# Forty up-projection pairs by Strassen's scheme on one core: seven half-size products, weight sums by adding transfers, g through DRAM, one separate down-projection

## The chip, the core and the metric

The kernel runs on one core of one Trainium2 chip. The metric is device time in microseconds (us) of the whole program, one launch. TensorE (PE in the profile) multiplies, VectorE (DVE), ScalarE (ACT) and GpSimd (POOL) work element by element, SyncE (SP) and GpSimd's queue (POOLq) issue transfers, which run on 16 DMA engines.

## The reference

One layer of a residual block, 512 tokens, width 2048, all in float32. The change touches its second sub-layer, the gated MLP:

```python
h2 = rmsnorm(x, ffn_pre_g)
up = causal_depthwise_conv(h2 @ w_up, conv_f_w, conv_f_b)      # w_up (2048, 11264), conv over 3 tokens
u_gate, u_val = jnp.split(up, 2, axis=-1)                      # 5632 columns each
f = (jax.nn.gelu(u_gate, approximate=True) * u_val) @ w_down   # w_down (5632, 2048)
x = x + rmsnorm(f, ffn_post_g)
```

Ahead of it stands a token-mixing sub-layer (w_in, w_a_out, w_b_out, w_o), behind it a per-layer embedding (w_ple, w_ple_gate). They are the same in both kernels.

## The kernel before

**Three products for one.** Every float32 matmul is made of three passes in the reduced type fp32r: an operand is split into a rounded high part and the rest, and high times high, high times low and low times high are summed in PSUM. Weights come in units of 128 partitions x 1024 float32 (512 KB; eight chunks of 128x128, or two of 128x512). For every unit ScalarE writes `w_hi` (`split`, L639), VectorE writes `w_lo = w_raw - w_hi` (`split`, L944), and TensorE makes 24 matmuls of it, 8 chunks x 3 (`products`, L400 to L402; `rows`, L466 to L468 for the down-projection). SyncE loads unit u when VectorE has split unit u-1 (two raw buffers); ScalarE splits unit u+4 when TensorE has finished unit u (four `w_hi` slots). So a split has about three units' time before TensorE wants it.

**The order of the work** is written out by hand, one program for each engine, with semaphores between them. The MLP goes over 44 column pairs, each a 128-wide column of the gate half and one of the value half, in 11 groups of four (`up`, then `down` for the group before). One column of 2048 rows is two units, 48 matmuls of 512 tokens; a pair is 96. Per column VectorE scales the PSUM tile by the token factors (`scale_tile`, L948), ScalarE makes the first tap of the convolution (L838), VectorE the other two (`last_taps`, L1275 and L1278). ScalarE makes the gelu (L843), VectorE the product (L1285); ScalarE (L834) and VectorE (L969) split the product g into high and low. Per group `down` multiplies four chunks of g by 8 units of w_down and VectorE adds the 16 PSUM tiles to `f_acc` (L1316), which GpSimd has set to zero (`memset`, L377).

**Ahead of the first pair** (`first_pair`) the second residual `x2` is turned by TensorE, squared row by row (L654), and its token factors go through four `diag` tiles (L959) and a matmul with ones (`spread`, L478). GpSimd stores `x2` in DRAM (L373), waits for it, and then sets `f_acc` to zero.

Of the kernel before, what the change touches and what calls it, by code (L numbers as in the profile page):

```python
# [34 lines left out]
P = 128  # L35
# [33 lines left out]
U_L = U_F + 4 * FC + 8 * NGRP  # L69
# [9 lines left out]
T_G = T_F + 2 * FC + DC * NGRP  # L79
F_UP = lambda j: U_F if j == 0 else U_F + 4 * GRP + 24 * (j - 1)  # L80
F_DOWN = lambda j: U_F + 4 * GRP + 24 * j + (4 * GRP if j < NGRP - 1 else 0)
FT_UP = lambda j: T_F if j == 0 else T_F + 2 * GRP + 24 * (j - 1)
FT_DOWN = lambda j: T_F + 2 * GRP + 24 * j + (2 * GRP if j < NGRP - 1 else 0)
# [15 lines left out]
C_ALL = C_CFW + FTAPS * 2 * FC  # L99

# [48 lines left out]
def build(nc, x, p, mix_pre_g, w_in, conv_a_w, conv_a_b, ln_a_g, ln_a_b, w_a_out, pool_w, pool_scale, w_b_out,  # L149
          w_o, mix_post_g, ffn_pre_g, w_up, conv_f_w, conv_f_b, w_down, ffn_post_g, w_ple, w_ple_gate,  # L150
          ple_post_g, out):
    x2_dram = nc.dram_tensor("x2_dram", (P, NG, BLK, W), F32, kind="Internal").ap()
    rows_of = lambda a: a.rearrange("a (b t) (n f) -> t n (a b) f", t=P, f=W)
    ctx = ExitStack()
    with ctx:
# [43 lines left out]
        g_hi = place("g_hi", [P, 2, GRP, TOK], F32R, r4)  # L199
        g_lo = place("g_lo", [P, 2, GRP, TOK], F32R, r4 + FULL // 2)  # L200
# [13 lines left out]
        gain_f = place("gain_f", [P, NG, W], F32, r2 + FULL - 4 * D)  # L214
# [8 lines left out]
        diag = small("diag", [P, BLK, P])  # L223
        r_bc = small("r_bc", [P, TOK])
        sq = small("sq", [P, 2, TOK])
# [4 lines left out]
        conv_acc = small("conv_acc", [P, TOK])  # L230
        sums = small("sums", [P, BLK, NG])
# [10 lines left out]
        raw_in = [sem(f"raw_in{s}") for s in range(RAW)]  # L242
        slots_freed = sem("slots_freed")
        hi_ready, lo_ready, units_done = sem("hi_ready"), sem("lo_ready"), sem("units_done")
# [19 lines left out]
        ff_ready, g_hi_ready, g_ready = sem("ff_ready"), sem("g_hi_ready"), sem("g_ready")  # L264
        ple_taken, y_ready = sem("ple_taken"), sem("y_ready")
        x_back, x2_out, f_zero = (sem(n) for n in ("x_back", "x2_out", "f_zero"))
# [9 lines left out]
        def _(sp):  # L276
            for_k = lambda w: w.rearrange("(k p) n -> p k n", p=P)
            win, wa, wb, wo = for_k(w_in), for_k(w_a_out), for_k(w_b_out), for_k(w_o)
            wup, wdn, wpg, wpl = for_k(w_up), for_k(w_down), for_k(w_ple_gate), for_k(w_ple)
# [15 lines left out]

            def pair(u, w, cols):

                for h in range(2):
                    for j in range(2):
                        half_column(u + (2 * h + j), w, cols[j], h)  # L300
# [33 lines left out]
            pair(At(F_UP(0)), wup, (0, FF))  # L334
            with sp.Fori(1, GRP) as c:
                column(At(F_UP(0), c, 4), wup, c * P)
                column(At(F_UP(0) + 2, c, 4), wup, c * P + FF)
            with sp.Fori(0, NGRP - 1) as j:
                for c in range(GRP):
                    column(At(F_UP(1) + 4 * c, j, 24), wup, j * (GRP * P) + (GRP + c) * P)  # L340
                    column(At(F_UP(1) + 4 * c + 2, j, 24), wup, j * (GRP * P) + ((GRP + c) * P + FF))
                for n in range(NG):
                    for v in range(GRP // 2):
                        rows(At(F_DOWN(0) + 2 * n + v, j, 24), wdn, j * GRP + 2 * v, n)
            with sp.Fori(0, NG) as n:
# [14 lines left out]
        def _(pool):  # L360
# [1092 lines left out]
```

## Time and profile before

| | us |
|---|---|
| median of 3 runs | 2665.03 |
| lowest, highest | 2664.44, 2666.41 |
| span of the profiled execution | 2665.0 |

| engine | busy us | share of the span | instructions |
|---|---|---|---|
| TensorE, matmul | 2637.8 | 99% | 11714 |
| TensorE, weight load | 2184.9 | 82% | 11714 |
| VectorE | 1348.2 | 51% | 1693 |
| ScalarE | 806.5 | 30% | 972 |
| GpSimd | 13.5 | 1% | 34 |

The span of the profiled execution equals the median, so a sum made against the profile needs no correction. The DMA engines move 277 MB, 104 GB/s on the mean. Weight loads have a row of their own (PEld) and overlap the matmuls. The recorded duration of a matmul (389 ns) is its latency; matmuls follow each other faster than that, and the distance of their starts is what counts.

### The profile page before, as it was taken

Reading aid. Unit: us, or ns where it says so; the run is one execution under the profiler, and the core shown is the slowest. Engines: PE = TensorE matmul, PEld = TensorE weight load, DVE = VectorE, ACT = ScalarE, POOL = GpSimd, SP = SyncE. Lnnn points to the kernel's source line nnn. Section 1 sums busy time; section 2 is a strip of 40 time slices with the busy share of each in tenths; the row PEclk is TensorE's granted clock in tenths of the full one; section 3 lists DMA queues with packets and bytes.
Section 4 is the critical chain, followed back from the end, with each engine's and each line's share of the span. In section 5 each row is a group of like instructions: output and inputs, shape, how many; then the busy total and the mean of one; then the engine's idle time right before and its main releaser. Section 6 shows DMA issues by size and latency. Waiting matters only on the chain.

```text
span 2665.0 us, 31629 instructions
## 1 busy us (share of the span) xinstructions
PE 2637.8 (99%) x11714; PEld 2184.9 (82%) x11714; DVE 1348.2 (51%) x1693; ACT 806.5 (30%) x972; POOL 13.5 (1%) x34
## 2 busy tenths in 40 slices
PE   8999999999999999999999999999999999999998
PEld 7888888888888877888888888888888888888886
DVE  6888766643334237444445444444454444446534
ACT  5222322342223234332323232222222222224423
POOL 0000000000000001000000000000000000000000
PEclk9999999999999999999999999999999999999999
DMA  5333333333334324333333333333333333343332
GB/s 163 103 95 100 98 95 99 91 115 99 95 95 161 100 79 150 95 95 98 100 95 95 97 101 96 95 96 101 96 95 96 101 97 95 96 172 103 104 103 103
DMA packets 384842, 277.26 MB, mean 104 GB/s; under 512 B 8116, under 2 KB 337500, under 8 KB 383708
## 3 DMA queue, kind: packets, MB, share of 16 engines
q1 hardware_dynamic: 380512, 259.03, 32.3%
q0 software_dynamic: 1296, 12.06, 1.2%
q10 hardware_dynamic: 2924, 4.54, 0.5%
q8 instruction: 89, 1.46, 0.2%
q14 instruction: 21, 0.17, 0.0%
HBM read 267.21 MB, written 8.39 MB: 103 GB/s over the span
## 4 chain that ended last, share of the span: by engine, by line
PE 98%; DVE 1%; ACT 1%; DMA 0%; issue 0%; DVEq 0%; ACTq 0%
PE ps L400 22%; PE ps L402 22%; PE ps L401 22%; PE ps L466 10%; PE ps L468 10%; PE ps L467 10%; PE ps L428 1%; ACT squares_out L654 0%; DVE e_buf L977 0%; DVE diag L959 0%; DMA x_nat<-in_x 0%; PE ps L478 0%; ACT xg_hi L659 0%; DVE x L977 0%; DVE w_lo L944 0%
## 5 line engine op out<-in xcount | busy, mean ns | idle before, releaser
L944 DVE TENSOR_TENSOR w_lo<-w_raw,w_hi 128x1024 fp32r<-128x1024 f32 x478 | 585.0, 1225 | 1186.1 <-ACT w_hi L639 1185.6
L400 PE MATMUL ps<-xg_hi,w_hi 128*128 128x512 f32 x2304 | 899.6, 390 | 1.6 <-DVE w_lo L944 1.6
L402 PE MATMUL ps<-xg_hi,w_lo 128*128 128x512 f32 x2304 | 898.1, 390 | 0.0
L401 PE MATMUL ps<-xg_lo,w_hi 128*128 128x512 f32 x2304 | 898.0, 390 | 0.0
L639 ACT ACTIVATE w_hi<-w_raw 128x1024 fp32r<-128x1024 f32 x478 | 506.0, 1060 | 1129.7 <-PE ps L402 599.2
L400 PEld LDWEIGHTS ps<-xg_hi,w_hi 128*128 128x128 f32 x2304 | 433.6, 188 | 92.5 <-issue 1.8
L402 PEld LDWEIGHTS ps<-xg_hi,w_lo 128*128 128x128 f32 x2304 | 433.5, 188 | 90.2
L401 PEld LDWEIGHTS ps<-xg_lo,w_hi 128*128 128x128 f32 x2304 | 433.6, 188 | 89.8
L466 PE MATMUL ps<-w_hi,g_hi 128*128 128x512 f32 x704 | 273.9, 389 | 0.0
L468 PE MATMUL ps<-w_lo,g_hi 128*128 128x512 f32 x704 | 273.9, 389 | 0.0
L467 PE MATMUL ps<-w_hi,g_lo 128*128 128x512 f32 x704 | 273.9, 389 | 0.0
L468 PEld LDWEIGHTS ps<-w_lo,g_hi 128*128 128x128 f32 x704 | 132.1, 188 | 27.5
L467 PEld LDWEIGHTS ps<-w_hi,g_lo 128*128 128x128 f32 x704 | 132.1, 188 | 27.4
L466 PEld LDWEIGHTS ps<-w_hi,g_hi 128*128 128x128 f32 x704 | 132.1, 188 | 27.3
L1316 DVE TENSOR_TENSOR f_acc<-f_acc,ps 128x512 f32<-128x512 f32 x176 | 109.0, 681 | 0.5 <-PE ps L468 0.5
L466 PE MATMUL ps<-w_hi,x_hi 128*128 128x512 f32 x256 | 99.9, 390 | 0.8 <-DVE x_lo L969 0.8
L466 PE MATMUL ps<-w_hi,xg_hi 128*128 128x512 f32 x256 | 99.7, 389 | 0.1
L468 PE MATMUL ps<-w_lo,x_hi 128*128 128x512 f32 x256 | 99.6, 389 | 0.0
L468 PE MATMUL ps<-w_lo,xg_hi 128*128 128x512 f32 x256 | 99.6, 389 | 0.0
L467 PE MATMUL ps<-w_hi,xg_lo 128*128 128x512 f32 x256 | 99.6, 389 | 0.0
L467 PE MATMUL ps<-w_hi,x_lo 128*128 128x512 f32 x256 | 99.6, 389 | 0.0
L1027 DVE SCALAR_TENSOR_TENSOR conv_acc<-a_conv,par,conv_acc 128x512 f32<-128x512 f32 x120 | 89.7, 748 | 0.0
(165 smaller groups left out, 1830.3 us busy)
## 6 DMA issues: line engine op xcount, KB each, us to landing
w_raw<-in_w_up SPq DMA_DIRECT2D x176, 512.0 KB, 3.9
w_raw<-in_w_in SPq DMA_DIRECT2D x112, 512.0 KB, 3.7
w_raw<-in_w_down SPq DMA_DIRECT2D x88, 512.0 KB, 3.7
w_raw<-in_w_o SPq DMA_DIRECT2D x32, 512.0 KB, 3.7
w_raw<-in_w_ple_gate SPq DMA_DIRECT2D x32, 512.0 KB, 3.7
w_raw<-in_w_b_out SPq DMA_DIRECT2D x16, 512.0 KB, 3.9
w_raw<-in_w_a_out SPq DMA_DIRECT2D x16, 512.0 KB, 4.0
x_nat<-in_x SPq DMA_DIRECT2D x4, 1024.0 KB, 9.6
```

Of the source, the lines that this page charges most:

```text
L400: pe.matmul(o, w_hi[:, s, cols], hi, start=start, stop=False)
L401: pe.matmul(o, w_hi[:, s, cols], lo, start=False, stop=False)
L402: return pe.matmul(o, w_lo[:, s, cols], hi, start=False, stop=stop)
L428: mm = pe.transpose(ps[:, bank0 + q, b * P:(b + 1) * P], src[:, n, b, q * P:(q + 1) * P], ident[:])
L466: pe.matmul(o, x_hi[:, k, tok], w_hi[:, s, cols], start=k == 0, stop=False)
L467: pe.matmul(o, x_lo[:, k, tok], w_hi[:, s, cols], start=False, stop=False)
L468: last = pe.matmul(o, x_hi[:, k, tok], w_lo[:, s, cols], start=False, stop=k == chunks - 1)
L639: f(w_hi[:, u.slot(SLOTS)], w_raw[:, u.slot(RAW)], ACT.Copy).then_inc(hi_ready, 1)
L944: dve.tensor_tensor(w_lo[:, s], w_raw[:, u.slot(RAW)], as_f32(w_hi[:, s]), ALU.subtract).then_inc(lo_ready, 1)
L1027: op(dve.scalar_tensor_tensor(out=both[k % 2], in0=chunk(k), scalar=weight, in1=both[k % 2], op0=ALU.mult, op1=ALU.add))
L1316: dve.tensor_tensor(f_acc[:, n, b], f_acc[:, n, b], ps[:, 4 * (n % 2) + b], ALU.add).then_inc(tiles_taken, 1)
```

## The change

**Layout.** The host hands w_up over in another order: unit by unit, so that each of the 128 rows of a transfer is 4 KB in one piece (no arithmetic).

**The first four pairs** are computed as before. Beside them VectorE makes four sums of halves of the activations (`s1`, `s2`, `s3`, `s7`, each 128 x 8 x 256) in nine instructions of 2048 columns, and splits each with ScalarE: four `low_sum` of 2048 columns on VectorE, four copies on ScalarE. TensorE waits for all four (`s_split`) before it goes on.

**The other 40 pairs** go by the Strassen-Winograd scheme. Activations are cut by halves of the 2048 rows and by halves of the 512 tokens, a pair's weights into gate and value column and halves of the rows. In place of eight products of a unit with 256 tokens (four units x 512 tokens) there are seven: W22, W11, T1, T2, T3, T4, W21. W22, W11 and W21 are units of w_up. T1 is a sum of two, T2 of three, T3 of two, T4 = T2 + W21. T1, T2 and T3 are made while they are loaded: SyncE loads one unit, GpSimd's queue issues a transfer that adds the next to it in SBUF (`add_unit`, four of them for a pair). VectorE makes T4 (`fourth_sum`). Raw units now live in a ring of ten buffers (`ring_raw`), which also hold the low parts; a buffer is loaded again when TensorE has finished the unit ten earlier. VectorE combines the seven PSUM results, with the copy `p1` that ScalarE makes, in seven instructions of 256 columns, and scales gate and value in SBUF.

**g through DRAM.** The product g is no longer split at once but stored (`g_dram`, 256 KB for a pair), read back in 11 pieces of 1 MB and split then (`quad_high`, `quad_low`). The down-projection stands behind all pairs, in four passes over 3, 3, 3 and 2 of these pieces; `f_acc` takes 64 PSUM tiles in place of 176, the first pass by copy, so the memset of `f_acc` is gone. All loops of this part are unrolled.

```diff
+W22, W11, T1, T2, T3, T4, W21 = range(PRODUCTS)
+RING = 10
+PASSES = (3, 3, 3, 2)
...
+            def ring_free(n):
+                if n < 4:
+                    sp.wait_ge(squares_ready, Q_O + DC)
...
+                else:
+                    sp.wait_ge(units_done, U_S + n - RING + 1)
...
+            for g in range(NS):
+                n, gate, val = PRODUCTS * g, GRP + g, FC + GRP + g
+                load_unit(n + W22, w_up[val, 1])
+                load_unit(n + W11, w_up[gate, 0])
+                load_unit(n + T1, w_up[val, 0])
+                load_unit(n + T2, w_up[val, 0])
+                load_unit(n + T3, w_up[val, 0])
+                load_unit(n + W21, w_up[gate, 1])
...
+            for g in range(NS):
+                n = PRODUCTS * (g + 1)
+                if g < NS - 1:
+                    add_unit(n + T1, w_up[GRP + g + 1, 0])
+                    add_unit(n + T2, w_up[GRP + g + 1, 0])
+                    add_unit(n + T3, w_up[FC + GRP + g + 1, 1])
+                    add_unit(n + T2, w_up[FC + GRP + g + 1, 1], second=True)
+                if g > 0:
+                    store_product(GRP + g - 1)
...
-            nc.gpsimd.memset(f_acc[:], 0.0).then_inc(f_zero, 1)
...
+                for k in range(HC):
+                    cols = slice(k * P, (k + 1) * P)
+                    pe.matmul(o, w_hi[:, s, cols], hi(k), start=k == 0, stop=False)
+                    pe.matmul(o, w_hi[:, s, cols], lo(k), start=False, stop=False)
+                    mm = pe.matmul(o, w_low[:, cols], hi(k), start=False, stop=k == HC - 1)
+                mm.then_inc(units_done, 1)
+
+            pe.wait_ge(s_split, 4)
+            for g in range(NS):
+                for idx in range(PRODUCTS):
+                    product(g, idx)
...
+                if c == GRP - 1:
+                    fourth_sum(0)
+                    low_sum(s2_lo, s2_raw, s2_hi, 2)
+                step(u + 3)
...
+                if c == GRP - 1:
+                    low_sum(s3_lo, s3_raw, s3_hi, 3)
```

VectorE in the third and fourth pair, before (L944 is the weight split, L1275 and L1278 the taps, L1285 the product, L969 the low part of g, L948 the scaling):

```order
L944 TENSOR_TENSOR w_lo<-w_raw,w_hi 128x1024 [waits hi_ready]
L1275 SCALAR_TENSOR_TENSOR gate_c<-up_gate,par,gate_c 128x512 [waits first_tap_ready]
L1278 SCALAR_TENSOR_TENSOR gate_c<-up_gate,par,gate_c 128x512 [waits dve_chain]
L944 TENSOR_TENSOR w_lo<-w_raw,w_hi 128x1024 [waits hi_ready]
L948 TENSOR_TENSOR up_val<-ps,r_bc 128x512
```

The same place now (L1223 and L1228 are the weight split, L1612 to L1622 the activation sums `s2` and `s3`, L1254 the low part of a sum):

```order
L1560 SCALAR_TENSOR_TENSOR gate_c<-up_gate,par,gate_c 128x512 [waits first_tap_ready,tiles_taken]
L1564 SCALAR_TENSOR_TENSOR gate_c<-up_gate,par,gate_c 128x512 [waits dve_chain]
L1612 TENSOR_TENSOR s_raw<-xg_lo,s_raw 128x2048 [waits s_ready]
L1614 TENSOR_TENSOR s_raw<-s_raw,xg_hi 128x2048 [waits dve_chain]
L1223 TENSOR_TENSOR w_lo<-w_raw,w_hi 128x1024 [waits hi_ready]
L1620 TENSOR_TENSOR s_raw<-xg_lo,s_raw 128x2048 [waits s_ready]
L1622 TENSOR_TENSOR s_raw<-s_raw,xg_hi 128x2048 [waits dve_chain]
L1233 TENSOR_TENSOR up_val<-ps,r_bc 128x512
L1228 TENSOR_TENSOR ring_lo_145<-ring_raw_135,w_hi 128x1024 [waits hi_ready]
L1560 SCALAR_TENSOR_TENSOR val_c<-up_val,par,val_c 128x512 [waits first_tap_ready,tiles_taken]
L1564 SCALAR_TENSOR_TENSOR val_c<-up_val,par,val_c 128x512 [waits dve_chain]
L1573 TENSOR_TENSOR gelu_g<-gelu_g,val_c 128x512 [waits gelu_ready,dve_chain]
```

Four instructions of 2048 columns stand between the taps of the third pair and the first weight split for the new scheme; the four low parts follow among the splits of the fourth pair.

VectorE in one of the 40 pairs now, from the results of one pair to those of the next (L1584 is `fourth_sum`, L1672 and L1722 combine the gate tile, L1714 the value tile):

```order
L1714 TENSOR_TENSOR up_val<-ps,v_115 128x256
L1716 TENSOR_TENSOR up_val<-up_val,r_bc 128x512 [waits c_taken]
L1584 TENSOR_TENSOR ring_raw_136<-ring_raw_144,ring_raw_137 128x1024 [waits units_done,ring_in2,ring_added9]
L1228 TENSOR_TENSOR ring_lo_153<-ring_raw_143,w_hi 128x1024 [waits hi_ready]
L1722 TENSOR_TENSOR up_gate<-ps,v_116 128x256 [waits c_taken,units_done]
L1672 TENSOR_TENSOR up_gate<-ps,p_113 128x256 [waits units_done]
L1228 TENSOR_TENSOR ring_lo_154<-ring_raw_144,w_hi 128x1024 [waits hi_ready]
L1677 TENSOR_TENSOR up_gate<-up_gate,r_bc 128x512 [waits c_taken]
L1560 SCALAR_TENSOR_TENSOR val_c<-up_val,par,val_c 128x512 [waits first_tap_ready,val_scaled]
```

The sum for T4 waits for adding transfers and stands ahead of a weight split in VectorE's queue.

## Rows read from the trace of the kernel before

**Rows 1.** The page: busy time and its share, by engine.
```profile
PE 2637.8 (99%) x11714; PEld 2184.9 (82%) x11714; DVE 1348.2 (51%) x1693; ACT 806.5 (30%) x972; POOL 13.5 (1%) x34
```
**Rows 2.** The page: chain that ended last.
```profile
PE 98%; DVE 1%; ACT 1%; DMA 0%; issue 0%; DVEq 0%; ACTq 0%
```
**Rows 3.** Timeline of TensorE, middle of the pairs: start, duration, engine, line.
```profile
1399.95 0.39 PE L400 MATMUL ps<-xg_hi,w_hi 128*128 128x512 f32 x1
...
1402.67 0.39 PE L400 MATMUL ps<-xg_hi,w_hi 128*128 128x512 f32 x1
```
**Rows 4.** Groups by form: line, xcount, busy us, mean ns, idle before.
```profile
L466 PE MATMUL ps<-w_hi,g_hi 128*128 128x512 f32 x704 | 273.9, 389 | 0.0
L540 PE MATMUL ps<-acc,ones 128*128 128x512 f32 x2 | 1.0, 592 | 0.0
```
**Rows 5.** Timelines of TensorE and its weight loads, at `spread` and at two float32 matmuls.
```profile
46.88 0.86 PEld L478 LDWEIGHTS ps<-diag,ones 128*128 128x128 f32 x7
...
499.32 1.02 PE L540 MATMUL ps<-acc,ones 128*128 128x512 f32 x2
...
532.86 0.86 PEld L546 LDWEIGHTS ps<-ones,acc 128*128 128x128 f32 x7
```
**Rows 6.** Timeline ahead of and at the first pairs: VectorE, TensorE, GpSimd, ScalarE.
```profile
1024.54 1.92 ACT L654 ACTIVATE squares_out<-x 128x2048 f32<-128x2048 f32 x1
...
1026.79 6.94 POOL L377 MEMSET f_acc<- 128x8192 f32 x1 [12.25 <-DMA x_dram<-x]
...
1027.12 7.13 DVE L959 TENSOR_SCALAR diag<-ident,rstd 128x128 f32<-128x128 f32 x4
...
1031.30 1.06 ACT L639 ACTIVATE w_hi<-w_raw 128x1024 fp32r<-128x1024 f32 x1 [1.76 <-DMA w_raw<-in_w_up]
...
1034.31 2.08 PE L478 MATMUL ps<-diag,ones 128*128 128x128 f32 x8 [3.30 <-DVE diag L959]
...
1036.45 0.68 DVE L965 COPY r_bc<-ps 128x512 f32<-128x512 f32 x1
...
1057.49 0.69 DVE L948 TENSOR_TENSOR up_val<-ps,r_bc 128x512 f32<-128x512 f32 x1
...
1098.13 1.06 ACT L639 ACTIVATE w_hi<-w_raw 128x1024 fp32r<-128x1024 f32 x1 [1.01 <-PE ps L402]
```
**Rows 7.** Stretches: us, busy of each engine, PEclk, DMA share, GB/s.
```profile
1016.00:1024.00 8.00, 8.00 (x43) 6.86 (x42) 3.91 (x6) 7.82 (x9) 0.00 (x0) 1.00 0.99 404
1033.40:1040.20 6.80, 5.89 (x18) 5.02 (x19) 5.83 (x12) 2.10 (x2) 0.32 (x1) 0.50 0.49 139
```
**Rows 8.** Timeline of VectorE in the pairs, middle of the kernel.
```profile
1403.96 1.23 DVE L944 TENSOR_TENSOR w_lo<-w_raw,w_hi 128x1024 fp32r<-128x1024 f32 x1 [2.58 <-ACT w_hi L639]
1405.11 0.68 DVE L948 TENSOR_TENSOR up_val<-ps,r_bc 128x512 f32<-128x512 f32 x1
...
1410.62 0.75 DVE L1275 SCALAR_TENSOR_TENSOR val_c<-up_val,par,val_c 128x512 f32<-128x512 f32 x1
...
1412.39 0.69 DVE L1285 TENSOR_TENSOR ff_prod<-gelu_g,val_c 128x512 f32<-128x512 f32 x1
...
1415.99 0.68 DVE L969 TENSOR_TENSOR g_lo<-ff_prod,g_hi 128x512 fp32r<-128x512 f32 x1
1416.59 0.69 DVE L948 TENSOR_TENSOR up_gate<-ps,r_bc 128x512 f32<-128x512 f32 x1
```
**Rows 9.** Groups of ScalarE between 1100 and 2380 us.
```profile
L639 ACT ACTIVATE w_hi<-w_raw 128x1024 fp32r<-128x1024 f32 x235 | 249.3, 1061 | 477.3 <-PE ps L468 263.9 <-PE ps L402 208.9 <-DMA w_raw<-in_w_down 4.5
L838 ACT ACTIVATE val_c<-up_val,par 128x512 f32<-128x512 f32 x41 | 33.4, 816 | 83.4 <-DVE up_val L948 83.4
L843 ACT ACTIVATE gelu_g<-gate_c 128x512 f32<-128x512 f32 x40 | 25.3, 632 | 114.1 <-DVE gate_c L1278 114.1
```
**Rows 10.** DMA issues: xcount, KB each, median us to landing.
```profile
w_raw<-in_w_up SPq DMA_DIRECT2D x176, 512.0 KB, 3.9
...
x<-x_dram POOLq DMA_DIRECT2D x4, 1024.0 KB, 5.1
```
**Rows 11.** Timeline of GpSimd: one issue of a transfer.
```profile
2369.49 0.53 POOL L384 DMA_DIRECT2D x<-x_dram  x1
```

More of the change, by code:

```diff
@@ L78 @@
 T_F = T_O + DC
[L79 to L83, printed above, removed]
+T_D = T_F + 2 * GRP
+T_G = T_D + DC * len(PASSES)
 EARLY = 7
@@ L99, with loads, adds, landed @@
 C_ALL = C_CFW + FTAPS * 2 * FC
+def loads(n):
+    return 1 if n >= N_DOWN or n % PRODUCTS != T4 else 0
+def adds(n):
+    return {T1: 1, T2: 2, T3: 1}.get(n % PRODUCTS, 0) if n < N_DOWN else 0
+def landed(n):
+    return 16 * sum(loads(m) for m in range(n % RING, n + 1, RING))
+def added(n):
+    return 16 * sum(adds(m) for m in range(n % RING, n + 1, RING))
 class At:
@@ L586, in _ @@
[L586 to L602 removed]
+            up(At(U_F), At(T_F), first=True)
@@ L604, in _ @@
+            for q in range(len(PASSES)):
+                for n in range(NG):
+                    if q == len(PASSES) - 1 and n == 1:
+                        pe.wait_ge(p_ready, PLEC)
+                    down(q, n)
             for n in range(NG):
@@ new lines, in _ @@
+            for c in range(GRP):
+                u = At(U_F + 4 * c)
+                if c == 0:
+                    step(u + 2)
+                    step(u + 3)
+                    tap_of_tile(gate_c, up_gate, c, 0)
+                    gelu(c)
+                else:
+                    step(u)
+                    step(u + 1)
+                    tap_of_tile(gate_c, up_gate, c, 0)
+                    step(u + 2)
+                    gelu(c)
+                    step(u + 3)
+                if c == 2:
+                    high_sum(s1_hi, s1_raw, 0)
+                    high_sum(s7_hi, s7_raw, 1)
+                tap_of_tile(val_c, up_val, c, 1)
+                if c == 2:
+                    high_sum(s2_hi, s2_raw, 2)
+                    high_sum(s3_hi, s3_raw, 3)
@@ new lines, in _ @@
+            for g in range(NS):
+                n, before = PRODUCTS * g, GRP + g - 1
+                if g > 0:
+                    step_ring(n - 1)
+                    val_tap(before)
+                    step_ring(n)
+                    gate_tap(before)
+                else:
+                    step_ring(n)
+                step_ring(n + 1)
+                if g > 0:
+                    act.wait_ge(c_taken, PRODUCTS * g)
+                f(p1[:], ps[:, W11, 0:TOKH], ACT.Copy).then_inc(p1_ready, 1)
+                step_ring(n + 2)
+                if g > 0:
+                    gelu(before)
+                step_ring(n + 3)
+                step_ring(n + 4)
+                if g == NS - 1:
+                    quad_high(0)
+                step_ring(n + 5)
```

620 lines of the change are left out of this document (439 added, 181 removed).

## The prediction

> **What bounds the kernel now.** I read the busy shares first [rows 1]: TensorE's matmuls fill 99% of the span, VectorE half of it, ScalarE 30%. The chain that ended last says the same: 98% of it is TensorE [rows 2]. So almost every us of matmul time taken away shows in the end, as long as nothing else becomes the limit, and almost every us in which TensorE idles is lost. How fast matmuls follow each other is read from a timeline: from 1399.95 to 1402.67 us there are 12 distances, so one matmul of 512 columns every 226.7 ns, although each is recorded with 389 [rows 3]. 512 columns at 2.4 GHz are 213.3 ns, so 13.4 ns come on top. The down-projection has the same form and the same 389 ns [rows 4]. The changed kernel keeps all of it but the 40 pairs, and alters what TensorE waits for at the two ends of them.
>
> **1. The products.** Removed are 40 pairs x 96 = 3840 matmuls of 512 columns: 3840 x 0.2267 = 870.5 us. Added are 40 x 7 x 24 = 6720 matmuls of 256 columns. The trace has no fp32r matmul of 256 columns, so their distance has to be bounded.
> - From below: each matmul brings a weight load. At L546 the matmuls have one column, so only the loads count: seven loads cover 0.86 us, and with 0.19 for the last that is 0.67/6 = 111.7 ns each [rows 5]. At `spread` (L478) seven loads take the same 0.86 us, and there the array works too: a float32 matmul of 512 columns takes 1.02 - 0.59 = 0.43 us per record [rows 4, 5], so one of 128 columns a quarter, 107 ns, just what 256 columns of fp32r take at 2.4 GHz. Load and array work of 107 ns each thus overlap at 111.7. Total 750.6 us.
> - From above: the 13.4 ns are a fixed price of a matmul: 106.7 + 13.4 = 120.1 ns, 807.1 us. If they grow with the columns instead, it is 113.4.
>
> I take 116 ns, about the middle, since no row tells fixed from growing: 779.5 us, 19.5 us for a pair where there were 21.8. The term is -91.0 us (bounds -119.9 and -63.4).
>
> The Trainium skill (TensorE: Matmul & The Clock Gate, section Back-to-back issue gap) gives columns/2.4 + 2.5 ns for a warm isolated matmul. By it 256 columns would take 109.2 ns, and the 512 of this kernel 215.8 where the row has 226.7; with 109.2 the term would be -136.7 us.
>
> **2. The start of the new scheme.** TensorE waits for the four split activation sums, and the last low part is behind the whole VectorE queue of pairs three and four. So I date that queue. A VectorE instruction of 512 columns is followed by the next after 0.60 us, one of 1024 after 1.15 [rows 8]; so 2.25 for 2048. Before, VectorE has scaled the second pair's value tile at 1057.5 + 0.6 = 1058.1 [rows 6]. That comes earlier now. The four `diag` took 7.1 us, with GpSimd's memset running all that time, and the memset is gone; but the next step still waits for a weight split that ScalarE ends at 1032.4, so `r_bc` comes at about 33.6 and not 36.45: 2.8 us. The absent splits of g (VectorE's low part, and ScalarE's copy ahead of its weight split) give about another 2.1 in this stretch, an estimate. So the queue below begins at 1053.2:
> - nine sums and four low parts, 13 x 2.25 = 29.3
> - eight weight splits, 8 x 1.15 = 9.2, and the fourth sum 1.15
> - four pairs of taps, 1410.62 to 1412.39, 4 x 1.77 = 7.1; two products 1.3; three scalings 1.8
> - waits for ScalarE: 2.0 in the third pair (tap and split), and 5.7 at the head of the fourth (tap 0.82, two copies of 2048 columns at 1.92, split 1.06) [rows 6, 9]
>
> That is 57.6 us, and TensorE starts at about 1110.8. Before, it goes on at 1098.1 [rows 6]. So +12.7 us, although the removed memset lets TensorE reach that point 6 us earlier: the 3.3 us idle at `spread` and the slow clock behind it are gained and lost again. TensorE idles some 18 us there. After the 3.3 us idle the granted clock was 0.50, the lower level, for 6.8 us [rows 7]; something like it will follow here, at half speed for 3.4 to 6.8 us, so 1.7 to 3.4 us lost: +2.5.
>
> **3. VectorE and ScalarE in a pair.** VectorE: seven splits 8.05, the fourth sum 1.15, seven instructions of 256 columns at 0.33 = 2.3, two scalings 1.2, four taps 3.5, the product 0.65: 16.9 us, with some 0.5 of waits on its own results 17.4 of 19.5. ScalarE: 7 x 1.06, two taps, gelu and a short copy, 10.0. Both fit, and a split may be about 5 us late before TensorE feels it. I cost them at 0. If that cover were gone, each us over 19.5 costs 40.
>
> **4. Transfers.** With DMA engines busy 0.99 they move 404 GB/s [rows 7], so 512 KB takes 524288/408000 = 1.29 us of all 16. A pair now has six loads, 7.7 us, the store of g, 0.65, and four adding transfers. No row shows one. It is at least a load (1.29, the second read hidden), and at most a load, a read back and a store (3.87). I take two loads, 2.57, since it reads two sources and its write overlaps as in any load. Sum 7.7 + 0.65 + 10.3 = 18.7 us of 19.5, hidden but close. The Trainium skill (Collectives: The Full Stack, section The bandwidth ceiling: the fold count and why AG ≠ RS ≠ AR) says that an add in a DMA engine reads two sources over the same read ring and so runs at half the rate of a copy; no run here shows it yet, and the sum would stay as it is.
>
> The longest chain is T2: loaded when the first unit of the pair before is done (2.8 us into it), two adds one behind the other. A load of 1.29 lands after 3.9, so 2.5 us of it are fixed (5.1 for 1024 KB) [rows 10]; issue on GpSimd is 0.5 [rows 11]. 2.8 + 3.9 + 2 x (2.57 + 2.5 + 0.5) = 17.8, with the adds for T1 and T3 between them about 19 to 20. VectorE wants it at about 17 for the fourth sum, and waits 2 to 3 us in which the weight split behind it waits too; TensorE needs that split at 19.5 + 5.6 = 25.1, so the sum may begin at 22.8 at the latest. Cost 0.
>
> **5. The start of the down-projection.** TensorE waits for the first piece of g, whose low part (2.25) VectorE makes when the last pair is done: +2. The 2112 matmuls stay, 479 us. The adds to `f_acc` and the splits of g lie beside TensorE in either kernel: 0. The weights' order in DRAM: 0, the loads were hidden. The end is the same: 0.
>
> **The sum.** 2665.0 - 91.0 + 12.7 + 2.5 + 2 = 2591.2 us. The profiled span equals the median of the runs.
>
> **The rivals.**
> A. *Adding transfers are dearer*, and the DMA engines set the pair's time, 8.4 + 4 x price. From 2.8 us each (2.2 loads) they pass TensorE's 19.5; from 21.3 us a pair, a price of 3.2 (2.5 loads), the change loses. At the upper bound, 3.87 each, a pair takes 23.9 us, 956 in all: 2665.0 + (956 - 870.5) + 17.2 = 2768 us, slower. For it: 18.7 of 19.5 leaves no room, and no row shows an add. Against: reads alone give two loads.
> B. *The load of weights doesn't overlap*: a load is recorded with 188 ns; if a matmul had to wait for all of it, 6720 x 0.188 = 1263 us, in all 3075. Against: at L546 and L478 loads recorded no shorter follow each other every 111.7 ns. Those are float32, not fp32r.
> C. *The in-order queues tie together*: T2 lands after 22.8, VectorE holds the splits behind it, and a pair takes perhaps 20.5 to 22 us, 2631 to 2691, around 2650.
>
> **How the numbers follow.** Forecast (TensorE sets the pair, 111.7 to 120.1 ns): 0.57, own range 2560 to 2623. A: 0.28, of it 0.05 at a price that still gains. B: 0.05. C: 0.10, of it 0.06 faster and 0.02 the same. Faster 0.57 + 0.05 + 0.06 less 0.02 for errors in the sum, 0.66; same 0.04; slower 0.30. About 0.2%, 5 us, is what a measurement of this kernel can tell from no change. The range goes from 2555 (112 ns and the start 5 us earlier) to 2775, just past A's bound; above stay B and an add dearer still, together 0.12, below 0.04.
>
> **What would show it.** TensorE's matmuls of 256 columns start every 112 to 120 ns with no idle between products, VectorE's busy share there is near 0.9, DMA share 0.9 or more: right. Idle before the first of the new matmuls near 18 us, released by a low part on VectorE: step 2 right. If ScalarE's split waits for a transfer and DMA share is 1.0, it is A; if distances are near 188 without idle time, B; if VectorE's fourth sum waits long for an add while DMA share is well under 1, C. The forecast falls if an add costs over 2.8 us, or if matmuls of half the columns don't come near half the time.

## The result and the profile after

The changed kernel takes **2690.2 us** (median of four runs, 2682.8 to 2697.6), the kernel before 2664.7: a ratio of **1.0098**, interval 1.0075 to 1.0121. It is 1% slower where 2591.2 and "faster" were forecast. The time lies in the stated range and in that of rival C (2631 to 2691), but on the slow side of the kernel before. The profiled execution took 2685.3 us and spans 2683.5, at the lower end of the runs.

The page of the changed kernel: busy shares, two lines of the 40 slices, and the chain by engine and by line.
```profile
PE 2591.7 (97%) x14594; PEld 2277.9 (85%) x14594; DVE 1560.4 (58%) x2001; ACT 924.9 (34%) x1103; POOL 174.5 (7%) x248
...
PEclk9999999999999999899999999999999999999999
DMA  5333333333334224699899999999962323242321
...
PE 76%; DMA 16%; DVE 4%; issue 2%; ACT 1%; POOL 0%; DVEq 0%; ACTq 0%; POOLq 0%; SPq 0%
DMA ring_raw<-in_w_up 15%; PE ps L538 10%; PE ps L540 10%; PE ps L539 10%; PE ps L794 6%; PE ps L795 6%; PE ps L796 6%; PE ps L745 5%; PE ps L609 5%; PE ps L610 5%; PE ps L611 5%; PE ps L747 5%; PE ps L746 5%; DVE ring_lo L1228 1%; ACT w_hi
```
Where TensorE had 98% of the chain [rows 2], it has 76%, and 15% is now transfers of up-projection weights into the ring. The rest says which transfers these are, and why they are late.

TensorE's timeline in the middle of a product, at the start of the scheme, at one of its idles, and at the start of the down-projection (start, duration, engine, line, in brackets the idle ahead and what ended it):
```profile
1399.95 0.28 PE L745 MATMUL ps<-s_hi,w_hi 128*128 128x256 f32 x1
...
1401.39 0.28 PE L745 MATMUL ps<-s_hi,w_hi 128*128 128x256 f32 x1
...
1106.52 0.58 PE L745 MATMUL ps<-s_hi,w_hi 128*128 128x256 f32 x1 [16.10 <-DVE s_lo L1254]
...
1504.88 0.55 PE L745 MATMUL ps<-s_hi,w_hi 128*128 128x256 f32 x1 [3.20 <-DVE ring_lo L1228]
...
1979.04 0.76 PE L794 MATMUL ps<-w_hi,q_hi 128*128 128x512 f32 x1 [7.85 <-issue]
```
The first two are 12 distances apart: 120.0 ns each. Over the 6523 undisturbed distances of the scheme (under 140 ns) the mean is 119.1 ns, so the products need 6720 x 0.1191 = 800.4 us, 20.0 a pair. (The expectations below were written with 118.85 ns, 798.7 us and a loss of 66 us, which is a little off; the undisturbed distances of every later kernel give 119.1 too.) The scheme's matmuls start from 1106.5 to 1970.9: 864.4 us, 21.6 a pair. So 64.0 us are lost inside it: 48 us in 24 places where two starts are 0.6 to 4.7 us apart, and 16 us of slower matmuls (most of them 0.21 us apart) behind such idles, where the granted clock is at its lower level. From here on an idle of TensorE is the distance of two starts; the figure in a line's bracket is up to 0.4 us shorter. The stretch behind the idle at 1504.88 has 0.57 in the clock's column:
```profile
1504.80:1508.40 3.60, 3.52 (x18) 3.56 (x19) 3.60 (x6) 1.57 (x3) 1.77 (x3) 0.57 0.82 151
```

The account of the 18.5 us by which the two spans differ: TensorE starts the last matmul of the fourth pair 7.7 us earlier (1090.0, 1097.7 before) and idles 16.5; the pairs take 864.4 for 870.5, so -6.1; the start of the down-projection costs 8.1 and 1.5 of slow clock; its matmuls follow each other after 228.9 ns for 226.7, 4.6 us; from its last matmul to the end it is 1.9 more. Together 18.8, which leaves 0.3 for rounding.

### The profile page after: what moved, and what is told of

The parts are those of the page before. It is cut to its first block, busy times and chain, and to the rows that moved or that the text cites. A ratio compares the mean times of both kernels' runs of the same rounds, so it can differ in the third digit from the quotient of the medians.

```text
span 2683.5 us, 36046 instructions
## 1 busy us (share of the span) xinstructions
PE 2591.7 (97%) x14594; PEld 2277.9 (85%) x14594; DVE 1560.4 (58%) x2001; ACT 924.9 (34%) x1103; POOL 174.5 (7%) x248
## 4 chain that ended last, share of the span: by engine, by line
PE 76%; DMA 16%; DVE 4%; issue 2%; ACT 1%; POOL 0%; DVEq 0%; ACTq 0%; POOLq 0%; SPq 0%
DMA ring_raw<-in_w_up 15%; PE ps L538 10%; PE ps L540 10%; PE ps L539 10%; PE ps L794 6%; PE ps L795 6%; PE ps L796 6%; PE ps L745 5%; PE ps L609 5%; PE ps L610 5%; PE ps L611 5%; PE ps L747 5%; PE ps L746 5%; DVE ring_lo L1228 1%; ACT w_hi L856 1%
## 5 line engine op out<-in xcount | busy, mean ns | idle before, releaser
L1228 DVE TENSOR_TENSOR ring_lo<-ring_raw,w_hi 128x1024 fp32r<-128x1024 f32 x404 | 492.8, 1221 | 410.4 <-ACT w_hi L856 409.9
L856 ACT ACTIVATE w_hi<-ring_raw 128x1024 fp32r<-128x1024 f32 x404 | 425.8, 1055 | 777.9 <-PE ps L796 343.8
L1223 DVE TENSOR_TENSOR w_lo<-w_raw,w_hi 128x1024 fp32r<-128x1024 f32 x194 | 237.0, 1224 | 410.0 <-ACT w_hi L846 409.6
L745 PE MATMUL ps<-s_hi,w_hi 128*128 128x256 f32 x1280 | 370.0, 289 | 60.3 <-DVE ring_lo L1228 44.2
L538 PE MATMUL ps<-xg_hi,w_hi 128*128 128x512 f32 x1024 | 399.6, 390 | 1.5 <-DVE w_lo L1223 1.5
L540 PE MATMUL ps<-xg_hi,w_lo 128*128 128x512 f32 x1024 | 398.5, 389 | 0.0
L539 PE MATMUL ps<-xg_lo,w_hi 128*128 128x512 f32 x1024 | 398.4, 389 | 0.0
L846 ACT ACTIVATE w_hi<-w_raw 128x1024 fp32r<-128x1024 f32 x194 | 204.9, 1059 | 529.9 <-PE ps L540 388.6
L747 PE MATMUL ps<-s_hi,ring_lo 128*128 128x256 f32 x1280 | 367.7, 287 | 0.0
L746 PE MATMUL ps<-s_lo,w_hi 128*128 128x256 f32 x1280 | 367.5, 287 | 0.0
L539 PEld LDWEIGHTS ps<-xg_lo,w_hi 128*128 128x128 f32 x1024 | 192.3, 188 | 39.7
```

The costliest lines, as they stand in the source:

```text
L538: pe.matmul(o, w_hi[:, s, cols], hi, start=start, stop=False)
L539: pe.matmul(o, w_hi[:, s, cols], lo, start=False, stop=False)
L540: return pe.matmul(o, w_lo[:, s, cols], hi, start=False, stop=stop)
L745: pe.matmul(o, w_hi[:, s, cols], hi(k), start=k == 0, stop=False)
L746: pe.matmul(o, w_hi[:, s, cols], lo(k), start=False, stop=False)
L747: mm = pe.matmul(o, w_low[:, cols], hi(k), start=False, stop=k == HC - 1)
```

## The experiments

Eleven kernels. `e1_no_adds`, `e3_t1_t3_no_add`, `e5_add_moved` and `e4_t2_by_vector` were run once each; the differences read from them are 60 us and more, four times the 15 us by which the changed kernel's own times differ. The others were run four to eleven times. "Stretch" is the time from the first matmul of the scheme to the last, 864.4 us in the changed kernel. In the cuts of code "..." marks what is left out.

### What makes the weights late

In the changed kernel all 24 idles of TensorE in the pairs stand at the same place, the first matmul of T1, and the same instruction ends them. Followed back from the one at 1504.88, which with 3.6 us is one of the longer ones (the chain of work in order of time: start, duration, what):
```profile
1478.88 4.39 DMA ring_raw<-in_w_up
1483.27 0.28 issue
1483.56 9.33 DMA ring_raw<-in_w_up
1492.89 0.28 issue
1493.17 9.18 DMA ring_raw<-in_w_up
1502.43 1.07 ACT w_hi L856
1503.51 1.23 DVE ring_lo L1228
1504.74 0.14 issue
1504.88 0.55 PE ps L745
```
This is T2's load and its two adding transfers, 23.5 us one behind the other. ScalarE's split in this chain is T2's own; it starts together with VectorE's fourth sum, and T1's high part had been ready since 1494. So VectorE's timeline beside it, where L1584 is the fourth sum and the L1228 behind it the split of the next pair's T1:
```profile
1492.88 0.69 DVE L1716 TENSOR_TENSOR up_val<-up_val,r_bc 128x512 f32<-128x512 f32 x1
1502.37 1.23 DVE L1584 TENSOR_TENSOR ring_raw<-ring_raw,ring_raw 128x1024 f32<-128x1024 f32 x1 [8.79 <-DMA ring_raw<-in_w_up]
1503.51 1.22 DVE L1228 TENSOR_TENSOR ring_lo<-ring_raw,w_hi 128x1024 fp32r<-128x1024 f32 x1
```
T2's load starts when W22's product is done, at 1478.88. Eight products later, after 22.8 us, TensorE stops: it wants T1. T1 had landed long before, but VectorE holds its low part behind the fourth sum, and that waits 8.8 us for T2. T2 itself would be wanted one product later, at 25.7.

The waits of the whole stretch (us in total, times, longest) say how regular this is: all 39 fourth sums wait, 5.1 us on the mean, and 24 times TensorE feels it. On the mean a fourth sum starts 22.1 us after the end of W22's product (19.7 to 24.9); the 23.5 above is one case.
```profile
ACT w_hi L856 <- DMA ring_raw<-in_w_up: 201.7, 33, 9.4
DVE ring_raw L1584 <- DMA ring_raw<-in_w_up: 198.5, 39, 9.8
PE ps L745 <- DVE ring_lo L1228: 44.2, 24, 4.4
```
But the DMA engines are nearly full too. So rivals A (their amount of work sets the pair) and C (the chain behind T2 and the queues do) both fit, and I made four kernels to part them. Their rows stand together below.

**No adding transfers at all** (`e1_no_adds`):
```diff
-    return {T1: 1, T2: 2, T3: 1}.get(n % PRODUCTS, 0) if n < N_DOWN else 0
+    return 0
...
             def add_unit(n, src, second=False):
 
+                return
```


> No adding transfers: the units T1, T2 and T3 hold their plain loads and not the weight sums (that part of the computation is left out; PE, VectorE and ScalarE do all that they did). Theories: (P) the 66 us that the scheme's stretch (1106.6 to 1971.0, 864.4 us) takes beyond its 6720 matmuls at 118.85 ns (798.7 us) all come from the weights' way in, be it work or latency: the stretch falls to 799-805 us and the run to 2625-2632 us. (V) they come from VectorE's and ScalarE's order of work: the stretch stays above 840 us and the run above 2665 us. I expect (P).

Measured: 2624.8 us, stretch 801.8, which is the first theory. All the loss is in the weights' way in; VectorE and ScalarE have time enough.

**Only T2's adds** (`e3_t1_t3_no_add`):
```diff
-    return {T1: 1, T2: 2, T3: 1}.get(n % PRODUCTS, 0) if n < N_DOWN else 0
+    return {T2: 2}.get(n % PRODUCTS, 0) if n < N_DOWN else 0
...
             def add_unit(n, src, second=False):
 
+                if not adds(n):
+                    return
```


> Only T2 keeps its two adding transfers; T1's and T3's are left out (those two sums are not made). Transfer work falls from about 20.5 us a pair (95% of the stretch) to about 15.1 us (70%), the chain behind T2 (load, add, add) keeps its three pieces. Throughput theory: the pieces get cheap as soon as the engines are not full, all the loss is gone, stretch 799-805 us, run 2625-2632. Chain theory: T2 still comes in three pieces of some 5 to 7 us each, so that ScalarE waits for it in part: stretch 805-835 us, run 2632-2662.

Measured: 2626.6 us, stretch 802.2, no idle. By itself this would speak for A: the chain has its three pieces, and nothing is lost. But the pieces got shorter with the load, 4.6 us for a load and 7.2 for an add (medians) where they were 6.3 and 8.3, and the fourth sum still waits 3.7 us a pair without TensorE noticing. It doesn't part the two.

**T2's second add given to W22** (`e5_add_moved`), all bytes kept:
```diff
-    return {T1: 1, T2: 2, T3: 1}.get(n % PRODUCTS, 0) if n < N_DOWN else 0
+    return {W22: 1, T1: 1, T2: 1, T3: 1}.get(n % PRODUCTS, 0) if n < N_DOWN else 0
...
                 if g < NS - 1:
+                    add_unit(n + W22, w_up[FC + GRP + g + 1, 1])
                     add_unit(n + T1, w_up[GRP + g + 1, 0])
                     add_unit(n + T2, w_up[GRP + g + 1, 0])
                     add_unit(n + T3, w_up[FC + GRP + g + 1, 1])
-                    add_unit(n + T2, w_up[FC + GRP + g + 1, 1], second=True)
```


> T2's second adding transfer goes to the unit W22, which is loaded first in its pair: as many transfers and bytes as before, four adds and six loads a pair, but no unit waits for more than load and one add (T2 and the product with W22 are not the scheme's sums). Throughput theory: 20.5 us of transfer work a pair are there as before, stretch 855-870 us, run 2680-2700. Chain theory: the longest chain is 6.2 + 8.3 us in place of 4.3 + 9.3 + 9.2, stretch 799-815 us, run 2625-2645.

Measured: 2625.3 us, stretch 803.0. This parts them. Six loads and four adds a pair are there as before, in less time, and inside the scheme TensorE never waits. The pieces are no shorter than in the changed kernel, where the medians are 6.3 us for a load and 8.3 for an add:
```profile
ring_raw<-in_w_up SPq DMA_DIRECT2D x231, 512.0 KB, 7.2
ring_raw<-in_w_up POOLq DMA_DIRECT2D x156, 512.0 KB, 8.5
```
So what helps is that no unit waits for three of them.

The last three kernels and the changed one, the same 800 us of each: the changed kernel, of `e5_add_moved`, `e3_t1_t3_no_add` and `e1_no_adds`, in this order (stretch, busy us of TensorE, its weight loads, VectorE, ScalarE, GpSimd; granted clock; DMA share; GB/s):
```profile
1108.00:1908.00 800.00, 761.10 (x6259) 756.81 (x6258) 592.64 (x808) 348.38 (x405) 147.84 (x185) 0.98 0.96 256
```
```profile
1108.00:1908.00 800.00, 800.00 (x6697) 800.00 (x6697) 655.92 (x873) 383.72 (x436) 158.05 (x199) 1.00 1.01 273
```
```profile
1108.00:1908.00 800.00, 800.00 (x6703) 800.00 (x6704) 639.16 (x873) 375.88 (x436) 91.20 (x121) 1.00 0.82 222
```
```profile
1108.00:1908.00 800.00, 800.00 (x6706) 800.00 (x6707) 661.73 (x873) 381.76 (x436) 23.30 (x43) 1.00 0.55 171
```
Read the share of DMA: 0.96 in the slow kernel, 1.01 in the fast one with the same bytes for each pair (the column adds the recorded times of packets up and can pass 1). A full DMA column isn't a bound by itself. It goes with a long chain, though: an add lands after 8.3 us here and after 5.6 where the engines have little else to do.

**The fourth sum behind T1's split** (`e6_sum_later`), nothing else changed:
```diff
+                split_ring(n + 9)
                 if g < NS - 1:
                     fourth_sum(n + PRODUCTS)
-                split_ring(n + 9)
```


> The changed kernel with all its transfers; only VectorE's order differs: the fourth sum stands behind the split of the next T1 and not ahead of it. In the trace of the changed kernel T2 lands 23.5 us after its load may start (4.4 + 9.3 + 9.2 and issues), VectorE's fourth sum waits 8.8 us for it, and TensorE idles 3.5 us for T1's low part, which is queued behind that sum, 22.8 us after that same point. Order theory: T1 is split in time, T2 itself is needed only at 25.7 us and is there with its two splits at 25.8, so at most a few tenths a pair are lost: stretch 800-815 us, run 2625-2645 us. Chain theory without the order (T2 is too late whatever VectorE does): the stretch gets shorter by less than half of 66 us, run 2655-2690.

Measured: 2662.9 us, ratio 0.9996 (0.9982 to 1.0011) to the kernel before, stretch 831.8. Half of the loss, 32.6 us of 64, goes with one statement on VectorE. By its numbers that is the second case at its very edge; the chain says why so much stays. (VectorE's L1722 is the last difference of the gate, L1672 the next pair's first gate sum.)
```profile
1503.89 6.20 DMA ring_raw<-in_w_up
1510.09 0.28 issue
1510.38 7.92 DMA ring_raw<-in_w_up
1518.29 0.28 issue
1518.58 8.95 DMA ring_raw<-in_w_up
1527.59 1.11 issue
1528.69 0.42 DVE up_gate L1722
1529.11 0.33 DVE up_gate L1672
1529.44 1.14 DVE ring_lo L1228
1530.59 0.14 issue
1530.72 0.36 PE ps L745
```
Now T2 itself is late: 23.6 us of transfers, then the fourth sum (1.1, the "issue" at 1527.59 here; it reads T2's raw buffer, which T2's low part overwrites, and so must come ahead of its split), 0.75 for two short instructions that I had left out, and the split, 26.8 in all against 25.7. So the loss had two parts of about equal size: the order, and the length of T2's chain.

**T2 made by VectorE** (`e4_t2_by_vector`) from the finished T1 and the raw W22, with no load and no add of its own:
```diff
-    return {T1: 1, T2: 2, T3: 1}.get(n % PRODUCTS, 0) if n < N_DOWN else 0
+    return {T1: 1, T3: 1}.get(n % PRODUCTS, 0) if n < N_DOWN else 0
...
-                load_unit(n + T2, w_up[val, 0])
...
-                    add_unit(n + T2, w_up[GRP + g + 1, 0])
                     add_unit(n + T3, w_up[FC + GRP + g + 1, 1])
-                    add_unit(n + T2, w_up[FC + GRP + g + 1, 1], second=True)
...
+            def second_sum(n):
+
+                sum_unit(n + T2, n + T1, n + W22)
...
+                if g < NS - 1:
+                    second_sum(n + PRODUCTS)
                 split_ring(n + 7)
```


> T2 is made by VectorE from T1 and the raw W22 (one sum of 1024 columns, 1.2 us) before W22 is split; its load and both adds go. Transfers fall by 1.3 + 5.4 us a pair to about 13.8 us (65%), VectorE rises from 16.0 to 17.2 us of a pair's 20. Both theories (throughput, chain) give a stretch of 799-812 us and a run of 2625-2640 us, below the kernel before (2664.7). A third, that VectorE's order of work becomes the bound (T2's sum waits for T1's add, and the splits of W22 and W11 are queued behind it), gives a stretch of 820-860 us and 2650-2690.

Measured: 2623.9 us, stretch 802.2, TensorE without an idle inside the scheme. One instruction of 1.2 us replaces three transfers (a load and two adds, 7.1 us of DMA work a pair by the prices in step 4 below); VectorE is busy 17.5 of 20 us:
```profile
1108.00:1908.00 800.00, 800.00 (x6702) 800.00 (x6703) 698.32 (x912) 382.06 (x436) 91.21 (x121) 1.00 0.72 197
```

### The two ends of the scheme

With T2 by VectorE the pairs are at TensorE's pace, and what is left are 16.6 us of idle ahead of them and 7.7 behind.

**The first piece of g ahead of the last store but one** (`e7_quad_first`, on top of `e4_t2_by_vector`):
```diff
+                if g == NS - 1:
+                    pool.wait_ge(units_done, last + W22 + 1)
+                    load_quad(0, 0)
                 if g > 0:
                     store_product(GRP + g - 1)
...
-            pool.wait_ge(units_done, last + W22 + 1)
-            load_quad(0, 0)
```


> T2 by VectorE as before (run at 2623.9), and on GpSimd the load of the first piece of g stands ahead of the last store but one of g, which waits 18.6 us for VectorE's product. It can start some 9 us earlier, at about 1892.7 in place of 1902.7. If the 7.7 us that TensorE idles ahead of the down-projection (1910.1 to 1917.7) and the half clock behind them (1.7 us) come from that load, the gap falls under 1.5 us and the run to 2614-2617 us. If VectorE's and ScalarE's queues at the end set it, less than 4 us are won: 2620-2624.

Measured: 2617.8 us, 0.9819 (0.9804 to 0.9834), just above the 2614 to 2617 of the first case. First TensorE's first matmul of the down-projection in `e4_t2_by_vector`, then in this kernel:
```profile
1917.74 0.77 PE L789 MATMUL ps<-w_hi,q_hi 128*128 128x512 f32 x1 [7.40 <-issue]
```
```profile
1912.87 0.47 PE L790 MATMUL ps<-w_hi,q_hi 128*128 128x512 f32 x1 [2.11 <-issue]
```
So most of it was the load of g from DRAM, queued on GpSimd behind a store that waited 18.6 us for VectorE. 2.1 us stay.

**Sums s2 and s3 on GpSimd** (`e8_sums_on_gpsimd`, on top of `e7_quad_first`): the four instructions of `sum_2` and `sum_3` move from VectorE's list to GpSimd's.
```diff
-                if c == 2:
-                    sum_2()
...
-                if c == 2:
-                    sum_3()
...
                     add_unit(T3, w_up[FC + GRP, 1])
+                    for k, (raw, prev, half) in enumerate(((s2_raw, s1_raw, slice(0, HC)), (s3_raw, s2_raw, slice(HC, DC)))):
+                        pool.wait_ge(s_ready, 2 + k)
+                        nc.gpsimd.tensor_tensor(out=raw[:], in0=xg_lo[:, half, 0:TOKH].bitcast(F32), in1=prev[:], op=ALU.subtract).then_inc(pool_chain, 1)
+                        pool.wait_ge(pool_chain, k + 1)
+                        nc.gpsimd.tensor_tensor(out=raw[:], in0=raw[:], in1=xg_hi[:, half, 0:TOKH].bitcast(F32), op=ALU.add).then_inc(s_ready, 1)
```

> As e7_quad_first, and the four instructions of 2048 columns that make the sums s2 and s3 run on GpSimd and not on VectorE. TensorE idles 16.5 us ahead of the scheme for VectorE's queue. Theory of the queue: VectorE has 4 x 2.29 = 9.2 us less, TensorE starts 5 to 9 us earlier, run 2605-2611 us. Rival: GpSimd takes over 6 us for each, or holds VectorE up as its memset seemed to do in the kernel before (four 128-column instructions in 7.1 us); then the gap stays or grows and the run is 2614-2640 us. I know no time of such a sum on GpSimd from this case; 0.5 for each.

Measured: 2630.9 us, 0.987 (0.9855 to 0.9885), and the idle is 30.3 us. The rival was right, by its second branch. TensorE's wait, GpSimd's first sum, and VectorE's second sum (T2) beside GpSimd's next:
```profile
PE ps L747 <- DVE s_lo L1256: 29.9, 1, 29.9
```
```profile
1078.46 4.91 POOL L489 TENSOR_TENSOR s_raw<-xg_lo,s_raw 128x2048 f32<-128x2048 f32 x1
```
```profile
1083.57 5.56 DVE L1588 TENSOR_TENSOR ring_raw<-ring_raw,ring_raw 128x1024 f32<-128x1024 f32 x1 [9.06 <-DMA ring_raw<-in_w_up]
```
GpSimd takes 4.5 to 5.4 us for 2048 columns where VectorE takes 2.29, so the four end at 1098.1. VectorE's 1024 columns take 5.56 us instead of 1.23 while GpSimd works from 1083.45 to 1088.05.

**The order around the start** (`e9_start_order`, on top of `e7_quad_first`): no instruction more or less. Shown are the first lines of VectorE's new order and TensorE's waits; ScalarE's splits are put into the same order.
```diff
+                if c == GRP - 1:
+                    second_sum(0)
+                    low_sum(s1_lo, s1_raw, s1_hi, 0)
+                    low_sum(s3_lo, s3_raw, s3_hi, 3)
+                    split_ring(0)
+                    split_ring(1)
+                    scale_tile(up_gate[:, 2:], At(T_F + 2 * c), bank=2 * c)
...
+                    if idx in (W22, T2, T3):
+                        pe.wait_ge(s_split, {W22: 2, T2: 3, T3: 4}[idx])
...
-            pe.wait_ge(s_split, 4)
```


> As e7_quad_first (2617.8), nothing added or removed, only orders. VectorE and ScalarE around the start of the scheme: the low parts of s1 and s3 fill the 4.3 us in which VectorE waited for a weight split (1084.2 to 1088.5), and s3's low part, which the first product needs, and the first weight splits come ahead of taps, product and scalings that nobody waits for; TensorE waits for each sum's low part where it uses it. At the end the first piece of g is split ahead of the last two weight splits. If the 16.4 us of idle ahead of the scheme are VectorE's order of work and not its amount, TensorE starts at 1091 to 1095 in place of 1107.5, the work put off fits in the 7 us that VectorE idles from 1111 to 1122, and the run is 12 to 18 us shorter: 2600-2606, ratio 0.976. If VectorE's amount of work sets it, the idle comes back inside the first pair and the run is 2610-2618.

Measured: 2608.5 us, 0.979 (0.9777 to 0.9803): 9.3 us won, between my two cases. The 16.4 us of idle are gone, the products follow the fourth pair at once; but a new one of 9.2 us comes at 1111.2. The waits of TensorE, and GpSimd's timeline:
```profile
PE ps L743 <- DVE up_val L1737: 9.0, 1, 9.0
```
```profile
1103.53 0.58 POOL L474 DMA_DIRECT2D g_dram<-gelu_g  x1 [19.75 <-DVE gelu_g L1574]
1107.45 0.57 POOL L474 DMA_DIRECT2D g_dram<-ff_prod  x1 [3.33 <-DVE ff_prod L1574]
1108.01 1.85 POOL L469 DMA_DIRECT2D ring_raw<-in_w_up  x2
```
GpSimd can't issue T1's add for the second pair before it has stored the g of pairs three and four, and I had just made those late. VectorE's second sum then waits 7.0 us for that add.

**The adds ahead of one store, and of both** (`e10_adds_first`, `e12_adds_ahead`):
```diff
-                store_product(c)
+                if c < GRP - 2:
+                    store_product(c)
...
+                if g == 0:
+                    store_product(GRP - 2)
+                    store_product(GRP - 1)
```
That is `e12_adds_ahead`; `e10_adds_first` moves only the second of the two stores.

> As e9_start_order, where TensorE now idles 9.2 us at 1111.2: VectorE's sum for the second pair's T2 waits 7 us for T1's adding transfer, which GpSimd issues only behind the store of the fourth pair's g, whose product VectorE now makes late (1106.5 to 1107.1). Only change: GpSimd issues the second pair's two adding transfers ahead of that store. If that queue is the cause, the idle goes with its slow clock and the run is 9 to 12 us shorter: 2597-2600, ratio 0.975. If VectorE's amount of work is behind it as well, 3 to 8 us of idle stay: 2601-2607.

> As e10_adds_first, where 5.7 us of idle are left at 1110.9: the adds were issued at 1103.8, behind the store of the third pair's g, whose product VectorE makes at 1102.3. Only change: both stores stand behind the second pair's adds. T1's add can then be issued when its load has landed, about 1096, and VectorE's sum finds it done at 1108.4. Queue theory: the idle falls under 1 us, the run is 5 to 8 us shorter than 2605.4: 2597-2600. Amount theory: VectorE's work lasts to 1108.3 without a pause, so 1 to 3 us of idle stay: 2600-2603.

Measured: 2605.4 us, 0.9779 (0.9765 to 0.9792), with 5.7 us of the idle left, the second case; then **2599.8 us, 0.976 (0.9747 to 0.9774)** with 2.2 left. By the idle that is the "amount" case of the last expectation, while the time lies on the border of the two. This is the best kernel of the study, 2.4% under the kernel before. TensorE's longest wait in it, and its page:
```profile
PE ps L747 <- DVE up_val L1741: 1.9, 1, 1.9
```
```profile
PE 2572.8 (99%) x14594; PEld 2263.2 (87%) x14594; DVE 1617.6 (62%) x2041; ACT 931.3 (36%) x1103; POOL 105.9 (4%) x168
```

### The memset that the change takes away

**The kernel before with its memset later** (`b1_memset_later`):
```diff
+            pool.wait_ge(spread_done, 4)
             nc.gpsimd.memset(f_acc[:], 0.0).then_inc(f_zero, 1)
```


> The kernel before, with GpSimd's memset of the accumulator behind the third spread (it runs beside the second pair of the up-projection). In the trace of before VectorE's four diagonals take 7.1 us while the memset of 6.94 us runs, TensorE idles 3.3 us for them and then has the half clock. If the memset holds VectorE's diagonals up: they take under 1 us, the idle and the slow clock go, and the run is 5 to 8 us shorter (2657-2660, ratio 0.997-0.998). If they are that slow by themselves: no change (2665). VectorE work that then runs beside the memset may be slower, at no cost to TensorE.

Measured: 2660.1 us, 0.9978 (0.9969 to 0.9987). VectorE's four diagonals, 7.13 us in [rows 6], now take 0.88, the idle of 3.3 us at `spread` is gone:
```profile
1026.08 0.88 DVE L960 TENSOR_SCALAR diag<-ident,rstd 128x128 f32<-128x128 f32 x4
```
So the kernel before loses 6 us to its memset, which has nothing to do with Strassen's scheme. How much of that the changed kernel wins by having none, no run here shows: it wins at most these 6 us (it would then be slower by 1.2% and not 1.0% without them), and perhaps less, since TensorE waits 16.5 us for VectorE's queue behind it. In that queue the copy to `r_bc` stands at 1031.3 where it stood at 1036.45 before. The 2.4% of `e12_adds_ahead` hold up to 0.2% of this kind.

## Why the prediction was wrong, step by step

- **Step 1, the products: right in mechanism, 21 us mis-sized.** 119.1 ns lies inside the bounds of 111.7 and 120.1, but near the upper one, where I took 116: 800.4 us for 779.5. The 13.4 ns over the array's own time [rows 3] are nearly a fixed price of a matmul (12.4 are left at 256 columns), not one that grows with the columns. Rival B is out.
- **Step 2, the start: right in mechanism and within 4 us.** TensorE starts at 1106.5 where 1110.8 was forecast, idles 16.5 for 18, and VectorE's low part ends the wait. `b1_memset_later` shows that the diagonals were slow because of the memset, as the step assumed. What it didn't ask is whether VectorE's order was needed: `e9_start_order` has the instructions of `e7_quad_first` and no idle there, and of the 9.2 us that come up behind it `e12_adds_ahead` leaves 2.2.
- **Step 3: right.** `e1_no_adds` and `e4_t2_by_vector` run the pairs at TensorE's pace; VectorE is busy 16.5 and 17.5 us a pair.
- **Step 4, the transfers: this is the step that failed, in its second half.** The price was good. By queue, between 1108 and 1908 us (packets, MB, share of 16 engines), GpSimd's transfers and SyncE's loads take
```profile
q0 software_dynamic: 24272, 87.31, 56.0%
q1 hardware_dynamic: 32095, 116.89, 39.7%
```
A load of 0.524 MB is thus 0.524 x 39.7%/116.89 x 800 = 1.42 us of all engines. With the 37 stores of g (9.7 MB, taken at the same rate) off the first line, an add is 0.524 x 52.7%/77.6 x 800 = 2.85: two loads, as taken, both a tenth over my figures. The Trainium skill (Collectives: The Full Stack, section The bandwidth ceiling: the fold count and why AG ≠ RS ≠ AR) has an add at half the rate of a copy because of its two source reads; by that rule too, the trace agrees, with a ratio of 2.0. The pair's sum is 20.6 us of work where I had 18.7. If that set the pair, as rival A has it, it would be over TensorE's 20.0 and cost 25 us. `e5_add_moved` shows that it costs nothing: the same sum is still 20.2 there, above TensorE's 20.1 a pair. So the recorded times of packets, added up, are no bound. Most packets of 4096 bytes are recorded with 159 ns in a load and 328 in an add, in both kernels (the medians); 128 of them on 16 engines are 1.27 and 2.62 us, and a pair by these is 18.8 us, the forecast's sum. The rest comes from packets recorded longer, and they are not a matter of a full column: the mean for a load is 177 ns in the changed kernel, at a share of 0.96, and 212 in `e1_no_adds`, at 0.55.
  What failed is the latency, the time from issue to landing. I gave each piece of T2's chain what it takes in an idle machine: 3.9 us for a load and 5.57 for an add. The add alone does land in 5.6 us, here the first one of `e12_adds_ahead`, at 1076 us with quiet engines:
```profile
ring_raw<-in_w_up POOLq DMA_DIRECT2D x1, 512.0 KB, 5.6
```
  In the pairs the trace has 4.4 + 9.3 + 9.2 with 96% of the DMA engines taken. I had written "hidden but close" for the work and in the next paragraph sized the chain as if the engines were free. The chain at 1504.88 ends at 2.85 + 23.5 = 26.3 us of the pair in place of 19 to 20, and the limit that I had worked out, 22.8, was about right: it is passed by 3.5 us, and TensorE's starts are 3.6 apart there. On the mean the sum starts at 2.85 + 22.1 = 25.0. The loss in the pairs is 62 of the 92 us between the forecast and the profiled execution.
- **Rival C happened, with A's sign.** Its mechanism, its place (the fourth sum holds the splits behind it) and its time range were right. My mark for telling it from A, a DMA share well under 1, was wrong: the share was 0.96, and in these runs long pieces and a high share go together. By my list of signs I would have called it A; only `e5_add_moved` and `e6_sum_later` say that it isn't. Its chance of 0.10 was too low, since it needed only 3 us more on a chain that I had priced without any waiting. That the 2690.2 lies in the stated range of 2555 to 2775 is no merit of the forecast: the range was made wide for rival A, which did not happen. (Its lower end is 4 us under what its own terms, 112 ns and 5 us, give; nothing hangs on that.)
- **Step 5, the start of the down-projection: 2 us forecast, 8.1 and 1.5 of slow clock found.** I counted the low part of the first piece of g and left out its load, which GpSimd issues behind a store that waits for VectorE (`e7_quad_first`).
- **Not foreseen:** 4.6 us in the down-projection's matmuls, 228.9 ns apart for 226.7. No run here tells why; it is there in all kernels of the study that have the separate down-projection.

The terms together, on the span: 2591.2 + 20.9 (products) - 4.3 (start) + 61.5 (idles and slow clock in the pairs, less the 2.5 forecast) + 7.6 (step 5) + 4.6 + 1.9 (end) = 2683.4, against 2683.5. The four runs' median is 5.0 us above the 2685.3 of that execution; the runs differ by 15 us, where those of the kernel before differ by 2. That the idles differ in length from run to run would explain it, but only one execution has a trace.

## What to carry to other kernels

Price a transfer twice: once for the work it gives the DMA engines, and once for the time until it lands, and take the second at the load that the first implies. Where a unit needs several transfers one behind the other, one VectorE instruction on data that is there anyway can be worth three of them. And on every in-order queue ask what stands behind an instruction that waits: here one sum ahead of one split was worth 27 us, a store ahead of a load 6, two stores ahead of an add 9 (2608.5 to 2599.8).

## What the runs showed of the hardware

- With six loads and four adds a pair, the DMA engines were recorded busy at 1.01 of the time in `e5_add_moved` and TensorE never waited; at 0.96 in the changed kernel the same products took 8% longer (864.4 us for 803.0). The share does not tell whether transfers bound a kernel.
- From issue to landing, medians for 512 KB: an adding transfer 6.4 us at a DMA share of 0.72, 7.2 at 0.82, 8.3 at 0.96, 8.5 at 1.01; a plain load 3.8 at 0.55, 5.1 at 0.72, 4.6 at 0.82, 6.3 at 0.96, 7.2 at 1.01.
- GpSimd's memset holds VectorE's `tensor_scalar` up until it ends (7.13 us for 0.88), and GpSimd's `tensor_tensor` makes VectorE's 1.23 us into 5.56. The Trainium skill (SBUF — State Buffer, section Who interferes with whom) says that the two engines share a pair of ports under an exclusive lock, which `tensor_scalar` can take in its two-port modes, and that a VectorE instruction with two inputs in SBUF contends with a GpSimd instruction that reads SBUF; both traces agree with it. In the kernel before the first cost 6 us (`b1_memset_later`).
